# Layer 0's input comes transposed from the host: an fp32 decoder trunk on Trainium2, first tile and first weight chunks in halves

## The chip, the cores and the metric

The kernel runs on one core of one Trainium2 chip. The metric is the device time of one execution in microseconds; the median of three runs of the kernel before is 1779.86 us.

## The reference, cut to what matters

A two-layer decoder trunk in fp32 for 512 prompt positions and 8 x 4 sample positions, 544 rows of 1024 features:

```python
h = x @ w_in        # 2816 columns: 11 pieces of 256 (val, gate, q, k, v, ...)
glu = val * sigmoid(gate)                        # -> causal depthwise conv
A, B, C, D = retention(...), dilated_attention(...), conv_module(glu), spatial_gating(...)
x = LN(alpha * x + concat(A, B, C, D) @ w_out)
x = LN(alpha * x + hier_moe(x))                  # top-1 of 4 groups, top-2 of 8 experts
```

TensorE contracts over partitions, so x @ w_in needs x with its features on the partitions: xT.

## The kernel before

The rows are cut into five tiles (ROWS: four of 128 rows and one of 32). w_in comes in 11 chunks of 1024 KB (128 partitions x 8 feature blocks x 256 columns), w_out in 4 more. They go through a ring of five slots in the big SBUF buffer `arena` (`ring`, `SLOT`); the trace calls the transfers arena<-in_w_proj. Two chunks are mostly used as a pair (`JOBS`), as VAL with GATE and SQ with SK: for each tile and each of the 8 feature blocks one matmul 128x512 (`weigh`, line 595; line 600 for the tile of 32 rows), which the trace shows as two records. xT is one buffer of 8 blocks x 544 positions.

In layer 0 each x tile is loaded with the positions on the partitions (`x_load`, line 373). TensorE transposes its eight 128x128 blocks against an identity into two PSUM banks (`turn_tile`, line 580), ScalarE copies them into xT (`turn_out`, line 1104), and then the VAL/GATE matmuls of that tile run (`first_pair`). The order on TensorE: transposes of tiles 0 and 1, matmuls of tile 0, transposes of tile 2, matmuls of tile 1, and so on. Then `tile(SQ, 0)`, then the transposes of the gating product (line 656), which wait for POOL's `glu` (line 1841), and on.

SyncE issues all loads of weights and x on one queue in the order in which they are written: identity (columns 0 to 127 of `const`), x tiles 0 and 1, chunks VAL and GATE, x tiles 2 to 4, the rest of `const` (lifts `start`), SQ, SK, three pieces of the samples' key cache, then the parameters of the layer, of which ret_state is the last (line 431). POOL waits for `start` ahead of three small scatters (line 1823), and for all five parameter transfers (`par_in`) ahead of two memsets and the gating product, which also waits for ScalarE's last copy of GATE (line 1119). VectorE waits for `start` ahead of everything.

SV and RQ are released when TensorE has finished the last VAL/GATE tile, RK by the SQ/SK job, later cache pieces and chunks by other semaphores of TensorE and VectorE. At the end of the attention part x is loaded again from `x_in`, for the residual sum. The MoE part of each layer streams the experts' matrices of 2048 KB (arena<-in_w, line 490), each released by a matmul of the turn before on the same of three lanes. Layer 1 transposes its x on the chip as well.

## Time and profile before

| | |
|---|---|
| three runs | 1776.07, 1779.86, 1783.07 us |
| span of the profiled execution, first to last instruction | 1777.2 us |
| granted TensorE clock, mean | 0.900 |
| TensorE matmul busy | 1434.9 us (81%) |
| VectorE / ScalarE / POOL busy | 568.8 / 217.3 / 362.6 us |
| 16 DMA engines | 516.25 MB, mean 290 GB/s |

The profiled execution's own device time isn't listed beside its span; the span lies inside the three runs. Times in the trace count from the first instruction of the span. SPq is SyncE's queue, on which the transfers are issued; a transfer lands some time after its issue. PEld is TensorE's loading of the stationary operand, which overlaps the matmuls.

### The profile page before, as it was taken

Reading aid. Unit: us, or ns where it says so; the run is one execution under the profiler, and the core shown is the slowest. Engines: PE = TensorE matmul, PEld = TensorE weight load, DVE = VectorE, ACT = ScalarE, POOL = GpSimd, SP = SyncE. Lnnn points to the kernel's source line nnn. Section 1 sums busy time; section 2 is a strip of 40 time slices with the busy share of each in tenths; the row PEclk is TensorE's granted clock in tenths of the full one; section 3 lists DMA queues with packets and bytes.
Section 4 is the critical chain, followed back from the end, with each engine's and each line's share of the span. In section 5 each row is a group of like instructions: output and inputs, shape, how many; then the busy total and the mean of one; then the engine's idle time right before and its main releaser. Section 6 shows DMA issues by size and latency. Waiting matters only on the chain.

```text
span 1777.2 us, 37861 instructions
## 1 busy us (share of the span) xinstructions
PE 1434.9 (81%) x15465; PEld 880.0 (50%) x15465; DVE 568.8 (32%) x1226; ACT 217.3 (12%) x621; POOL 362.6 (20%) x513
## 2 busy tenths in 40 slices
PE   8989999979567656878498999998757798689870
PEld 4546875555234333445245578746434454355440
DVE  0766654341000000101458756535100011011117
ACT  2223210101000000000022230200000000001000
POOL 1000120023122221323110003110322233224322
PEclk9999999999788787989699999998988899899995
DMA  8242234378999999999850430617799999989993
GB/s 317 86 169 84 72 113 181 132 313 357 425 426 424 426 424 426 400 425 403 323 221 25 169 131 27 228 80 303 322 423 425 420 361 421 424 348 398 419 396 153
DMA packets 60985, 516.25 MB, mean 290 GB/s; under 512 B 12118, under 2 KB 15794, under 8 KB 32122
## 3 DMA queue, kind: packets, MB, share of 16 engines
q1 hardware_dynamic: 49834, 497.47, 68.5%
q0 software_dynamic: 11088, 17.89, 2.8%
q8 instruction: 45, 0.74, 0.2%
q14 instruction: 18, 0.15, 0.0%
HBM read 795.97 MB, written 27.46 MB: 463 GB/s over the span
## 4 chain that ended last, share of the span: by engine, by line
PE 52%; DMA 36%; DVE 6%; issue 2%; SPq 1%; ACT 1%; POOL 1%; POOLq 0%; DVEq 0%; ACTq 0%
DMA arena<-in_w 31%; PE ps L595 22%; PE ps L1036 14%; PE ps L1054 5%; DVE arena L1790 1%; PE ps L600 1%; DMA xT<-x1d,xT 1%; PE ps L700 1%; DMA arena<-in_w_proj 1%; PE ps L580 1%; DMA arena<-in_kv 1%; PE ps L718 1%; PE ps L949 1%; DVE bn L1536 1%; SPq L490 1%
## 5 line engine op out<-in xcount | busy, mean ns | idle before, releaser
L1036 PE MATMUL ps<-arena,xT 128*32 128x256 f32 x7104 | 469.4, 423 | 185.9 <-DMA arena<-in_w 184.6
L1036 PEld LDWEIGHTS ps<-arena,xT 128*32 128x32 f32 x7104 | 273.1, 122 | 369.9 <-issue 268.4
L595 PE MATMUL ps<-arena,xT 128*128 128x512 f32 (+1 forms) x1280 | 446.9, 504 | 2.7 <-DMA arena<-in_w_proj 1.1
L595 PEld LDWEIGHTS ps<-arena,xT 128*128 128x128 f32 x1280 | 245.9, 197 | 176.1 <-issue 152.4
L1758 DVE COPY xT<-ps 128x128 f32<-128x128 f32 x111 | 32.4, 292 | 836.5 <-PE ps L1045 836.5
L1054 PE MATMUL ps<-arena,xT 128*32 128x256 f32 x3552 | 219.0, 387 | 33.3 <-DVE xT L1758 25.5
L1054 PEld LDWEIGHTS ps<-arena,xT 128*32 128x32 f32 x3552 | 112.9, 111 | 111.8 <-issue 29.3
L1879 POOL DMA_INDIRECT xT<-x1d,xT x111 | 116.9, 1053 | 88.1 <-POOL xT L1877 84.8
L1889 POOL DMA_INDIRECT yd<-xT x111 | 113.3, 1021 | 91.4 <-POOL xT L1887 86.4
L1877 POOL COPY xT<-xT 128x1 int32 x111 | 20.5, 185 | 477.4 <-PE ps L1026 477.4
L1310 DVE SCALAR_TENSOR_TENSOR arena<-arena 128x784 f32<-128x784 f32 x120 | 115.3, 1028 | 0.0
L1225 ACT ACTIVATE xT<-ps 128x128 f32<-128x128 f32 x111 | 30.8, 278 | 603.8 <-PE ps L1036 603.8
L1835 POOL TENSOR_TENSOR rstat<-rstat,halfc 128x5 f32<-128x5 f32 (+2 forms) x6 | 14.9, 2484 | 331.2 <-DVE rstat L1272 331.2
L1230 ACT COPY xT<-ps 128x256 f32<-128x256 f32 x111 | 41.4, 373 | 289.9 <-PE ps L1054 289.9
L1116 ACT ACTIVATE arena<-ps 128x256 f32<-128x256 f32 x88 | 31.4, 383 | 301.9 <-PE ps L595 301.9
L580 PE MATMUL ps<-const,arena 128*128 128x128 f32 (+1 forms) x240 | 33.8, 289 | 33.4 <-DVE arena L1545 26.9
L1754 DVE COPY xT<-ps 128x256 f32<-128x256 f32 x117 | 49.7, 425 | 28.4 <-PE ps L1026 28.4
L1026 PE MATMUL ps<-const,xT 128*128 128x128 f32 x234 | 45.6, 277 | 15.2 <-DMA xT<-x1d,xT 14.1
L1863 POOL TENSOR_TENSOR mv<-mv,halfc 128x1 f32<-128x1 f32 (+1 forms) x10 | 15.2, 1519 | 175.0 <-DVE mv L1567 175.0
L580 PEld LDWEIGHTS ps<-const,arena 128*128 128x128 f32 (+1 forms) x240 | 28.6, 154 | 42.1 <-DVE arena L1545 27.9
L1104 ACT COPY xT<-ps 128x512 f32<-128x512 f32 (+1 forms) x50 | 24.8, 525 | 182.4 <-PE ps L580 182.1
L1045 PEld LDWEIGHTS ps<-const,xT 128*128 128x128 f32 x111 | 15.4, 138 | 45.7 <-issue 45.7
(257 smaller groups left out, 1099.5 us busy)
## 6 DMA issues: line engine op xcount, KB each, us to landing
arena<-in_w SPq DMA_DIRECT2D x333, 2048.0 KB
arena<-in_w_proj SPq DMA_DIRECT2D x30, 1024.0 KB, 7.7
arena<-in_kv SPq DMA_DIRECT2D x32, 640.0 KB, 7.5
arena<-yd SPq DMA_DIRECT2D x16, 512.0 KB, 6.9
rowpar<-in_rowpar SPq DMA_DIRECT2D x2, 2708.0 KB, 18.3
arena<-in_x_in SPq DMA_DIRECT2D x8, 512.0 KB, 5.0
x1d<-arena SPq DMA_DIRECT2D x8, 512.0 KB, 2.6
arena<-x1d SPq DMA_DIRECT2D x8, 512.0 KB, 13.3
```

The lines of the kernel that those rows point to most:

```text
L580: ins = pe.transpose(ps[g][:, j * 128:j * 128 + n], source(t, 4 * g + j), ident[0:n, 0:n])
L595: ins = pe.matmul(bank[0:n, 0:w * CW], xT[:, k, 128 * t:128 * t + n], columns(k, slice(0, CW)), start=(k == 0), stop=(k == KT - 1))
L1026: ins = pe.transpose(TOKENS[:, b * 128:(b + 1) * 128], xg[q][:, b * 128:(b + 1) * 128], ident)
L1036: ins = pe.matmul(HB[q][r, 0:256], xgT[q][:, k % 2, BLK * (k // 2):BLK * (k // 2 + 1)], w13[q][:, :, k, 128 * j:128 * (j + 1)], start=(k = ...
L1054: ins = pe.matmul(YB[q][r, 0:256], hT[q][:, BLK * c:BLK * (c + 1)], w2[q][:, c, 256 * t:256 * (t + 1)], start=(c == 0), stop=(c == 3), til ...
L1116: ins = act.activation(h[0:n, c, t, :], bank[0:n, at * CW:(at + 1) * CW], func.get(c, ACT.Copy))
L1230: act.copy(yo[q], YB[q][:, 0:256]).then_inc(sem(f"y_out{q}"), 1)
L1310: ins = dve.scalar_tensor_tensor(out=acc[:, cb, :], in0=src, scalar=cw[:, cb * TAPS + j:cb * TAPS + j + 1], in1=acc[:, cb, :], op0=ALU.mul ...
L1754: dve.tensor_copy(xgT[q], TOKENS[:, 0:256].rearrange("p (b m) -> p b m", b=2)).then_inc(sem(f"xgT{q}"), 1)
L1758: dve.tensor_copy(hT[q], HIDDEN[:, 0:128]).then_inc(sem(f"hT{q}"), 1)
L1879: pool.indirect_dma_start(out=xg[q], out_offset=None, in_=x1q, in_offset=bass.IndirectOffsetOnAxis(ap=gidx[q], axis=0), bounds_check=4 * N ...
L1889: pool.indirect_dma_start(out=ydq, out_offset=bass.IndirectOffsetOnAxis(ap=yidx[q], axis=0), in_=yo[q], in_offset=None, bounds_check=4 * ( ...
```

## The change

The host writes a second copy of x, `xT_in`, already transposed and laid out tile by tile: 128 partitions, and for each tile 8 feature blocks of as many columns as the tile has rows. xT in SBUF takes the same layout for both layers (`xT_tile`). In layer 0 the transposes and ScalarE's copies fall away. x tile 0 comes as two transfers of four feature blocks each, and so do the chunks VAL and GATE. The first halves lift the semaphore `early`, on which the first four matmuls wait; the other four of tile 0 wait for the second halves. `const` is loaded whole, behind SK; TensorE waits for it ahead of `tile(SQ, 0)`. POOL raises the counts of the semaphores of the transposes that fell away. In layer 0, SyncE's wait for the transposes ahead of the fourth cache piece (line 436) goes too. The reload of x for the residual sum stays.

Left out of the diff are lines that only say `xT_tile(t)` in place of a slice of xT (matmuls, router, VectorE's copy), the name of the flat view, and the final count.

```diff
@@ -164,6 +164,7 @@
 
+LOADED = dict(xT_tr=10, xT_low=5, xT_high=5)
 PER = dict(par_in=80, xT_tr=30, xT_low=15, xT_high=15, proj=40, proj_out=40,
@@ -193,7 +194,7 @@
 
-        xT = sb("xT", [128, KT, NTOK])
+        xT = sb("xT", [128, KT * NTOK])
         const = sb("const", [128, sum(n for _, n in const_at.values())])
@@ -207,6 +208,10 @@
         halfc = sb("halfc", [128, 4 * TILES])
+
+        def xT_tile(t):
+            at, n = KT * 128 * t, ROWS[t]
+            return xT[:, at:at + KT * n].rearrange("p (k n) -> p k n", k=KT)
 
@@ -367,13 +372,19 @@
             E = Eng(sp, "none")
-            sp.dma_start(const[:, 0:128], io["const"][:, 0:128]).then_inc(sem("ident"), 16)
-
-            def x_load(t):
-                sp.dma_start(x[0:ROWS[t], t, :], io["x_in"][128 * t:128 * t + ROWS[t], :]).then_inc(sem(f"x_in{t}"), 16)
-
-            x_load(0)
-            x_load(1)
+            HALF = KT // 2
+
+            def xT_load(t, a, b, name):
+                sp.dma_start(xT[:, a:b], io["xT_in"][:, a:b]).then_inc(sem(name), 16)
+
+            def first_half(c):
+                src = io["w_proj"][bass.ds(c, 1), :, 0:HALF * CW].rearrange("a p n -> (a p) n")
+                sp.dma_start(ring[slot(c)][:, 0:HALF].rearrange("p k c -> p (k c)"), src).then_inc(sem("early"), 16)
+
+            def second_half(c):
+                src = io["w_proj"][bass.ds(c, 1), :, HALF * CW:].rearrange("a p n -> (a p) n")
+                sp.dma_start(ring[slot(c)][:, HALF:].rearrange("p k c -> p (k c)"), src).then_inc(sem(f"ring{slot(c)}"), 16)
+
             def ring_fill(layer, c):
@@ -404,11 +415,14 @@
                 if L == 0:
-                    ring_load(0)
-                    ring_load(1)
-                    for t in range(2, TILES):
-                        x_load(t)
-                    sp.dma_start(const[:, 128:], io["const"][:, 128:]).then_inc(start_sem, 16)
+                    xT_load(0, 0, HALF * 128, "early")
+                    first_half(VAL)
+                    first_half(GATE)
+                    xT_load(0, HALF * 128, KT * 128, "x_in0")
+                    second_half(VAL)
+                    second_half(GATE)
+                    for t in range(1, TILES):
+                        xT_load(t, KT * 128 * t, KT * (128 * t + ROWS[t]), f"x_in{t}")
                 else:
@@ -416,6 +430,8 @@
                 ring_load(SK)
+                if L == 0:
+                    sp.dma_start(const[:], io["const"][:]).then_inc(start_sem, 16)
                 for i in range(NKV - 1):
@@ -433,8 +449,8 @@
 
-                        E.need("xT_tr", 2 * TILES)
                         if L:
+                            E.need("xT_tr", 2 * TILES)
                             sp.wait_ge(sem("x_saved"), L * 16 * TILES)
@@ -566,10 +582,9 @@
             ident = C("ident")
-            pe.wait_ge(sem("ident"), 16)
             for L in range(DEPTH):
                 E.L = L
-                turned = [0]
+                turned = [0 if L else TILES]
 
@@ -606,12 +621,18 @@
                     if part != 1:
+                        if j == 0 and L == 0:
+                            pe.wait_ge(sem("early"), 48)
+                            weigh(ps[2], chunks, t, range(KT // 2))
+                            pe.wait_ge(sem("x_in0"), 16)
                         if place == 0:
                     ks = range(KT) if part is None else range(part * KT // 2, (part + 1) * KT // 2)
+                    if j == 0 and L == 0:
+                        ks = range(KT // 2, KT)
                     ins = weigh(ps[2 + j % 2], chunks, t, ks)
@@ -633,22 +654,24 @@
                 def turn_x(t):
-                    pe.wait_ge(*((sem("x2"), (L - 1) * TILES + t + 1) if L else (sem(f"x_in{t}"), 16)))
+                    pe.wait_ge(sem("x2"), (L - 1) * TILES + t + 1)
                     turn_tile(t, x_block)
 
-                turn_x(0)
                 if L:
+                    turn_x(0)
                     first_pair(0)
                         first_pair(t, 1)
+                    first_pair(TILES - 1)
                 else:
-                    for t in range(1, TILES):
-                        turn_x(t)
-                        first_pair(t - 1)
-                first_pair(TILES - 1)
+                    for t in range(TILES):
+                        if t:
+                            pe.wait_ge(sem(f"x_in{t}"), 16)
+                        tile(VAL, t)
+                    pe.wait_ge(start_sem, 16)
                 tile(SQ, 0)
@@ -1094,14 +1117,14 @@
                 E.L = L
-                turned = [0]
+                turned = [0 if L else TILES]
 
                         src = ps[g][:, :].rearrange("p (j m) -> p j m", j=4)[:, :, 0:n]
-                        E.done(act.copy(xT[:, 4 * g:4 * g + 4, 128 * t:128 * t + n], src), ("xT_low", "xT_high")[g])
+                        E.done(act.copy(xT_tile(t)[:, 4 * g:4 * g + 4, :], src), ("xT_low", "xT_high")[g])
                     turned[0] += 1
@@ -1120,11 +1143,15 @@
 
-                for t in range(TILES):
-                    turn_out(t, (0, 1))
-                    if t:
-                        proj_out(VAL, t - 1)
-                proj_out(VAL, TILES - 1)
+                if L:
+                    for t in range(TILES):
+                        turn_out(t, (0, 1))
+                        if t:
+                            proj_out(VAL, t - 1)
+                    proj_out(VAL, TILES - 1)
+                else:
+                    for t in range(TILES):
+                        proj_out(VAL, t)
                 for t in range(TILES):
@@ -1809,6 +1836,8 @@
 
+            for name, n in LOADED.items():
+                pool.sem_inc(sem(name), n)
             pool.sem_inc(sem("yidx"), 1)
@@ -1967,8 +1996,10 @@
     colpar = c(np.concatenate([col[n].reshape(L, 128, -1) for n, _ in COLPAR], 2)).reshape(L * 128, -1)
+    rows_in = np.concatenate([a["x_prompt"].reshape(SEQ, D), a["x_sample"].reshape(NS, D)], 0)
+    xT_in = [rows_in[128 * t:128 * t + n].reshape(n, KT, 128).transpose(2, 1, 0).reshape(128, KT * n) for t, n in enumerate(ROWS)]
     return dict(
-        x_in=c(np.concatenate([a["x_prompt"].reshape(SEQ, D), a["x_sample"].reshape(NS, D)], 0)),
+        xT_in=c(np.concatenate(xT_in, 1)), x_in=c(np.concatenate([a["x_prompt"].reshape(SEQ, D), a["x_sample"].reshape(NS, D)], 0)),
         w_proj=w_proj, kv=kv.reshape(L * 16, 128, 2 * NKEY), rowpar=rowpar, colpar=colpar, router_w=router_w,
```

TensorE, from the start of the program. Before (x_in0 to x_in4 are the x tiles, ring0 and ring1 the slots of VAL and GATE, xT_low and xT_high ScalarE's copies):

```order
L580 MATMUL ps<-const,arena 128x128 [waits x_in0,ident]
L580 MATMUL ps<-const,arena 128x128 x7
L580 MATMUL ps<-const,arena 128x128 [waits xT_low,x_in1]
L580 MATMUL ps<-const,arena 128x128 x3
L580 MATMUL ps<-const,arena 128x128 [waits xT_high]
L580 MATMUL ps<-const,arena 128x128 x3
L595 MATMUL ps<-arena,xT 128x512 [waits ring0,ring1,xT_high,xT_low]
L595 MATMUL ps<-arena,xT 128x512 x7
L580 MATMUL ps<-const,arena 128x128 [waits xT_low,x_in2]
```

And with the change (its line 610 is line 595 of before, 615 is 600):

```order
L610 MATMUL ps<-arena,xT 128x512 [waits early]
L610 MATMUL ps<-arena,xT 128x512 x3
L610 MATMUL ps<-arena,xT 128x512 [waits ring1,ring0,x_in0]
L610 MATMUL ps<-arena,xT 128x512 x3
L610 MATMUL ps<-arena,xT 128x512 [waits x_in1]
L610 MATMUL ps<-arena,xT 128x512 x7
L610 MATMUL ps<-arena,xT 128x512 [waits proj_out,x_in2]
```

The transposes are gone, tile 0 is cut in two by its waits, and the other tiles wait for their x alone (and for the PSUM bank).

SyncE's queue, from its start. Before:

```order
L370 DMA const<-in_const 128x128
L373 DMA arena<-in_x_in 128x1024 x2
L379 DMA arena<-in_w_proj 128x2048 x2
L373 DMA arena<-in_x_in 128x1024 x2
L373 DMA arena<-in_x_in 32x1024
L411 DMA const<-in_const 128x2982
L379 DMA arena<-in_w_proj 128x2048
L379 DMA arena<-in_w_proj 128x2048 [waits pinit]
L404 DMA arena<-in_kv 128x1280 x3
```

And with the change:

```order
L378 DMA xT<-in_xT_in 128x512
L382 DMA arena<-in_w_proj 128x1024 x2
L378 DMA xT<-in_xT_in 128x512
L386 DMA arena<-in_w_proj 128x1024 x2
L378 DMA xT<-in_xT_in 128x1024 x3
L378 DMA xT<-in_xT_in 128x256
L390 DMA arena<-in_w_proj 128x2048
L390 DMA arena<-in_w_proj 128x2048 [waits pinit]
L434 DMA const<-in_const 128x3110
L415 DMA arena<-in_kv 128x1280 x3
```

The first transfers are now the ones of the first four matmuls; the constants have moved behind SQ and SK.

## Rows read from the trace of the kernel before

**Rows 1.** The page, its part 2: matmul busy tenths in 40 slices.
```profile
PE   8989999979567656878498999998757798689870
```
**Rows 2.** Chain of waits, first 60 us: start us, us, what.
```profile
2.57 8.75 DMA arena<-in_w_proj
...
11.45 9.10 PE ps L595 x16
20.55 0.87 PE ps L580 x8
21.43 6.87 PE ps L595 x16
28.30 0.87 PE ps L580 x8
29.17 6.87 PE ps L595 x16
36.04 0.61 PE ps L580 x8
36.65 7.06 PE ps L595 x16
43.72 1.89 PE ps L600 x64
45.60 7.06 PE ps L595 x16
52.66 0.45 PE ps L656 x4
```
**Rows 3.** Timeline of SyncE's queue, first issues: start us, us, engine, line, operation.
```profile
0.71 0.39 SPq L370 DMA_DIRECT2D const<-in_const  x1
1.16 0.90 SPq L373 DMA_DIRECT2D arena<-in_x_in  x2
```
**Rows 4.** DMA issues: x loads of line 373, and the identity (last figure: landing).
```profile
DMA to landing us min/median/max: 3.9/9.5/11.1
...
const<-in_const SPq DMA_DIRECT2D x1, 64.0 KB, 2.0
```
**Rows 5.** Busy time by stretch: engines, then granted clock, DMA share, GB/s.
```profile
2.00:3.00 1.00, 0.00 (x0) 0.00 (x0) 0.00 (x0) 0.00 (x0) 1.00 (x1) 1.00 0.90 145
...
6.00:11.00 5.00, 3.05 (x14) 2.27 (x12) 0.00 (x0) 3.53 (x5) 0.00 (x0) 1.00 1.00 418
```
**Rows 6.** Timeline of TensorE's weight loads in tile 0 of VAL/GATE.
```profile
15.00 0.34 PEld L595 LDWEIGHTS ps<-arena,xT 128*128 128x128 f32 x1 [0.52 <-issue]
15.67 0.19 PEld L595 LDWEIGHTS ps<-arena,xT 128*128 128x128 f32 x1 [0.34 <-issue]
16.10 0.19 PEld L595 LDWEIGHTS ps<-arena,xT 128*128 128x128 f32 x1 [0.24 <-issue]
```
**Rows 7.** Timeline of TensorE at the start of layer 1.
```profile
875.97 1.97 PE L580 MATMUL ps<-const,arena 128*128 128x128 f32 x8 [20.50 <-DVE arena L1545]
878.66 8.99 PE L595 MATMUL ps<-arena,xT 128*128 128x512 f32 x16 [0.72 <-issue]
```
**Rows 8.** Timeline of POOL and ScalarE, 18 to 54 us.
```profile
18.59 0.10 POOL L1819 MEMSET nowhere<- 128x1 int32 x1 [14.29 <-DMA const<-in_const]
...
39.17 0.15 POOL L1838 MEMSET arena<- 128x60 f32 x1 [15.78 <-DMA arena<-in_ret_state]
39.37 0.53 POOL L1839 MEMSET arena<- 128x512 f32 x1
47.56 2.88 POOL L1841 TENSOR_TENSOR arena<-arena 128x1280 f32<-128x1280 f32 x1 [7.66 <-ACT arena L1119]
...
45.67 1.81 ACT L1119 ACTIVATE arena<-ps 32x64 f32<-32x64 f32 x8 [1.26 <-PE ps L600]
```
**Rows 9.** Expert stage of layer 0: stretch (as rows 5), and a link of the chain.
```profile
400.00:860.00 460.00, 331.49 (x4836) 187.24 (x4828) 41.44 (x148) 32.23 (x99) 119.72 (x195) 0.85 0.99 413
...
444.22 37.30 DMA arena<-in_w
```

More of the change, by code:

```diff
@@ L483, in _ @@
                 E.need("stores", 16 * 9)
-                E.need("xT_tr", 20)
+                E.need("xT_tr", 4 * TILES)
                 E.need("smp_back", 1)
@@ L594, in weigh @@
                         if t < TILES - 1:
-                            ins = pe.matmul(bank[0:n, 0:w * CW], xT[:, k, 128 * t:128 * t + n], columns(k, slice(0, CW)),
+                            ins = pe.matmul(bank[0:n, 0:w * CW], xT_tile(t)[:, k, :], columns(k, slice(0, CW)),
                                             start=(k == 0), stop=(k == KT - 1))
@@ L948, in tile_logits @@
                     for k in range(KT):
-                        ins = pe.matmul(ps[6][0:n, t * NLOG:(t + 1) * NLOG], xT[:, k, 128 * t:128 * t + n], rw[:, k, :],
+                        ins = pe.matmul(ps[6][0:n, t * NLOG:(t + 1) * NLOG], xT_tile(t)[:, k, :], rw[:, k, :],
                                         start=(k == 0), stop=(k == KT - 1))
@@ L1915, in _ @@
                     E.done(pool.tensor_tensor(mv[0:n, t, 2:3], mv[0:n, t, 3:4], halfc[0:n, 0:1], ALU.pow), "x2_pow")
-    wrong = {name: (made.get(name, 0), n) for name, n in PER.items() if made.get(name, 0) != n * DEPTH}
+    wrong = {name: (made.get(name, 0), n) for name, n in PER.items() if made.get(name, 0) != n * DEPTH - LOADED.get(name, 0)}
     assert not wrong, wrong
```

6 lines of the change are left out of this document (3 added, 3 removed).

## The prediction

> **What bounds the kernel now.** I read the page's slices first. TensorE is busy in nine or eight tenths of nearly every slice, so no single stage stands out at a glance [rows 1]. The question is therefore only what the start-up costs and whether time saved there reaches the end. The chain of waits answers the first half [rows 2]: from 2.57 us the chain waits 8.75 us for the second weight chunk (landing at 11.32), and from 11.45 us it is TensorE without a break: five VAL/GATE tiles with the transposes of tiles 2, 3 and 4 between them, to 45.60, where the SQ/SK job begins. The chain has no ACT, POOL or DMA link between 11.45 and 52.66. So two things can be won: the wait ahead of 11.45 and the transposes inside the stretch. The two transposes ahead of 11.45 (tiles 0 and 1) lie under the wait for the weights and are worth nothing.
>
> The queue of SyncE shows why the weights land so late: the identity (64 KB) is issued at 0.71 and two x tiles from 1.16 on, ahead of the two chunks of 1024 KB [rows 3]. Sizes in KB are of 1024 bytes.
>
> **Term 1, when TensorE can start.** After the change it needs half of x tile 0 (256 KB) and two half chunks (512 KB each): 1280 KB = 1.311 MB, the first transfers in the queue. No row shows this transfer, so I bound it with two landings. x tile 0 landed 3.9 us after its issue at 1.16, at 5.06, with 64 + 512 KB = 0.590 MB asked for up to it [rows 3, 4]. The second chunk landed at 11.32 with 64 + 2 x 512 + 2 x 1024 KB = 3.211 MB [rows 2]. Between them 2.621 MB in 6.26 us: 0.419 MB/us, which is the 418 GB/s of the stretch from 6 to 11 us [rows 5]. On that line 1.311 MB lands at 5.06 + 0.721/0.419 = 6.78 us. The line holds the identity's cost: from 2 to 3 us the DMA engines were 0.90 busy and moved only 145 GB/s [rows 5], rows of 512 bytes; at 418 the same bytes take 0.35, so up to 0.65 us falls away, and I take 0.3. Bounds: 5.9 (all of it falls away, and a little of the interleaving behind x tile 0) and 6.9. I take **6.5**, and 0.13 us to the first matmul as now (11.32 to 11.45): 6.63.
>
> **Term 2, the first tile.** Its matmuls (two records each, 16 in all) start 0.85 us apart at first and 0.43 from 15.67 on [rows 6]: five records at TensorE's lower level of 1.2 GHz, eleven at 2.4, 9.10 us in all [rows 2], though the column of the granted clock says 1.00 there. Did the transposes of tiles 0 and 1 ahead of it help to raise the clock? At the start of layer 1 TensorE had been idle for 20.50 us, did only the 1.97 us of transposes and then the same tile in 8.99 us [rows 7]. Less work ahead, the same tile: I take 9.10 with nothing ahead of it. Bounds: 7.03, the 16 records all at 0.43 and the drain (a clock already high, for which nothing speaks), and 13.7, sixteen at 0.853. The second half of the tile waits for 2.621 MB (x tile 0 and both chunks whole): on the line 5.06 + 2.031/0.419 = 9.9 us. Its first half takes five records of 0.853 and three of 0.43, 5.56 us, to 12.2, so that wait costs nothing; if the clock were high at once, the first half would end at 10.1, and still no wait. Tile 0 ends at 6.63 + 9.10 = 15.73 instead of 20.55: **4.82 us**.
>
> **Term 3, the transposes in the stretch.** 0.87 + 0.87 + 0.61 = **2.35 us** go [rows 2]. What stays is 6.87 + 6.87 + 7.06 + 1.89 = 22.69. The x tiles that these wait for are issued after the halves: tile 1 is the 3.145th MB, 11.2 us on the line, and tile 4 the 4.325th, 14.0; TensorE asks at 15.7 and at 36.5. The five pairs of ScalarE's copies out of PSUM go too; they hid under matmuls. The SQ/SK job then starts at 15.73 + 22.69 = 38.42 instead of 45.60: **7.18 us** earlier.
>
> **What has moved behind it.** The constants, identity included, now stand behind SQ and SK. Their bytes and those ahead of them: x 2176 KB, four chunks 4096 KB, constants 1555 KB, together 7827 KB = 8.01 MB, 5.06 + 7.42/0.419 = 22.8 us. Readers: TensorE at 38.4 (a new wait, with 15 us to spare), VectorE not before its first copy (after 52.66 now), and POOL, whose three small scatters now follow at 18.59 [rows 8] and then idle for ret_state. All hidden. SyncE still waits for two of POOL's memsets ahead of SK, which are POOL's first work and no later than before. SQ and SK land by 19, before 38.4. SyncE issues two transfers more (three halves and no identity), some 0.45 us each as the first ones [rows 3]; it is far ahead of the DMA engines by then.
>
> ret_state is the last of the parameters, at 39.17 [rows 8], and the bytes ahead of it are the same: it stays at 39.1, because it is the DMA engines that set it. POOL then does its two memsets (0.15 and 0.53) and is free at 39.9. It needs ScalarE's last copies of GATE: now 45.67 + 1.81 = 47.5, then 40.3. So the gating product starts at 40.3 and ends 2.88 later at 43.2, and TensorE wants it at 52.66 - 7.18 = 45.48. Slack 2.3 us, as now (50.4 to 52.66). This is the one place where the fixed DMA time and the earlier TensorE meet; ret_state could be 1.5 us later and still cost nothing at all on TensorE.
>
> The new layout of xT, tile by tile, keeps each 128x128 block contiguous per partition; the copies and weight loads have the same shapes. I cost it at nothing: a weight load of 0.19 us lies under a matmul of 0.43 [rows 6].
>
> **Does it reach the end?** After 52.66 every transfer of layer 0 is released by a semaphore of TensorE or VectorE, and moves with it. The expert stage is where it could be lost: from 400 to 860 us the DMA engines are 0.99 busy at 413 GB/s, and the chain goes through loads of up to 37.30 us [rows 9]. But the load issued before 444.22 was released by a matmul of the turn before, and the streamed bytes are fixed: a stream that starts 7.18 us sooner ends 7.18 us sooner. So the sum is 4.82 + 2.35 = 7.2 us (0.4%) off the profiled execution with its span of 1777.2, which lies within the three runs shown (median 1779.86). From the median: 1779.86 - 7.2 = **1772.7**.
>
> **Rivals.**
> A, the halves don't overlap. The lone 64 KB transfer took 2.0 us from issue to landing [rows 4]; if each of the three early pieces paid that in series, they would land at 0.71 + 6.0 + 1.311/0.419 = 9.8, tile 0 would end at 19.1, and the gain would be 3.8: 1776.1. Against it: x tiles and chunks, issued 0.45 apart, moved at a steady 418 GB/s [rows 5]. Chance 0.06. The Trainium skill speaks for this rival, "DMA: Bandwidth & Descriptors", section Bandwidth: transfers should be batched to a mebibyte or more, and the fit on the same page (2.0 us + bytes at 436 GB/s each) would give the three in series 9.0 us, so a landing at 9.7, an estimate from that page. The trace disagrees so far as it goes, with its 418 GB/s over queued transfers of 512 and 1024 KB.
> B, the clock stays low through the first tile, since nothing precedes it: 16 x 0.853 = 13.65, 4.55 more, gain 2.6: 1777.2. Against it the restart [rows 7]. Chance 0.12 with what lies halfway.
> C, all goes well: landing at 5.9, clock up after three records, gain 7.2 + 0.6 + 0.9 = 8.7, and up to 9.6 if the second half's landing (9.9, and 3.4 of matmuls) sets it: 1770.3 to 1771.2. Chance 0.10.
> D, the gain is absorbed downstream: the expert stage waits on bytes, and if its stream were already at its limit before its first turn, nothing would arrive: 1779.9. Against it: its loads wait for TensorE's turns. Chance 0.10. This is also how it looks if scatter covers it, since the runs before span 7.0 us by themselves.
> E, slower. The new pieces (rows of 1 to 4 KB out of longer rows) move as badly as the identity did, 145 GB/s instead of 418: 4.325 MB take 29.8 us instead of 10.3, so ret_state lands at 58.6, the gating product ends at 58.6 + 0.8 + 2.88 = 62.3, and TensorE, which now wants it at 52.66, stands: 9.6 us lost, 1789.5. It decides from a ret_state later than 52.66 - 2.88 - 0.8 = 49.0, which is 214 GB/s for those pieces. Against it: the present x tiles already are rows of 4 KB, at 418. Chance 0.03.
>
> **The numbers.** My forecast has 0.59. The gain is set beside a median of runs that lie 7.0 us apart, so I allow 2 to 3 us on either side of the cases: **1768.5 to 1777.5** takes in A, B and C and leaves out most of D and E. A measurement of this kernel can tell about 0.5% from no change, 8.9 us. Faster by more: C with luck, and the forecast with scatter, 0.21. Slower by more: E, 0.03. Within: 0.76.
>
> **What the changed profile would show.** First matmul near 6.6 us; records 0.85 apart for some 4 us, then 0.43; no pause between the halves; SQ/SK starting near 38.4; POOL's product ending before TensorE asks (no wait of matmuls at the transposes of VAL); ret_state still at 39; the first experts some 7 us sooner. I would be wrong if TensorE waited for POOL near 45 us, if the first tile took over 11 us, or if the stage from 400 us did not move with the start.

## The result and the profile after

The changed kernel takes 1765.55 us (median of 4 runs, 1764.52 to 1768.49), and the kernel before, taken beside it, 1779.59 (4 runs, 1776.07 to 1783.07): a ratio of 0.9919, 95% interval 0.9898 to 0.9940, so 14 us or 0.8% faster. The forecast was 1772.7 with 1768.5 to 1777.5. The sign is right, and the size is about half of what came: 7.2 us forecast, 14 measured. The profiled execution took 1764.52 us, with a span of 1762.7. One run of the kernel of experiment 10 took 2785.49 us where its five others took 1765.42 to 1768.04; it is left out below.

The page, its first part and the matmul slices of part 2, stand like this after the change; matmuls are busy 1422.3 us where the trace of before has 1434.9:

```profile
span 1762.7 us, 37770 instructions
...
PE 1422.3 (81%) x15425; PEld 871.3 (49%) x15425; DVE 568.5 (32%) x1226; ACT 212.5 (12%) x611; POOL 360.3 (20%) x513
...
PE   8989999888577656887498999998857798599880
```

**The start.** The chain of waits of the changed kernel (start us, us, what) answers to [rows 2]:

```profile
1.63 6.55 DMA arena<-in_w_proj
...
8.22 29.32 PE ps L610 x64
37.54 1.88 PE ps L615 x64
39.43 7.06 PE ps L610 x16
46.49 0.45 PE ps L679 x4
```

The halves land at 8.18 and the first matmul starts at 8.22 instead of 11.45. From there TensorE runs without a break and the SQ/SK job starts at 39.43 instead of 45.60: 6.17 us earlier, where 7.18 were forecast. The four full tiles take 29.32; without 6.87 + 6.87 + 7.06 for tiles 1 to 3 [rows 2], tile 0 took 8.52. That the tiles 1 to 3 are as before is seen on ScalarE, whose copies of the tiles out of PSUM now follow each other at 6.87 us (before 7.75 and 7.67, with the transposes between):

```profile
30.71 0.66 ACT L1139 ACTIVATE arena<-ps 128x256 f32<-128x256 f32 x2 [6.21 <-PE ps L610]
37.58 0.66 ACT L1139 ACTIVATE arena<-ps 128x256 f32<-128x256 f32 x2 [6.21 <-PE ps L610]
```

The landing is late because the DMA engines move less than they did. Busy time by stretch of the changed kernel (PE, PEld, DVE, ACT, POOL, then granted clock, DMA share, GB/s), beside [rows 5]:

```profile
3.00:4.00 1.00, 0.00 (x0) 0.00 (x0) 0.00 (x0) 0.00 (x0) 1.00 (x3) 1.00 0.91 270
4.00:5.00 1.00, 0.00 (x0) 0.00 (x0) 0.00 (x0) 0.00 (x0) 0.30 (x1) 1.00 0.77 283
5.00:6.00 1.00, 0.00 (x0) 0.00 (x0) 0.00 (x0) 0.00 (x0) 0.00 (x0) 1.00 0.98 338
6.00:11.00 5.00, 2.78 (x4) 1.23 (x5) 0.00 (x0) 0.00 (x0) 0.00 (x0) 1.00 0.97 318
```

From 6 to 11 us it is 318 GB/s, where the kernel before moved 418 in the same stretch. The engines are nearly as busy (0.97 and 1.00): they are not short of work, each piece takes longer.

The weight loads of tile 0 answer to [rows 6] (timeline: start us, us, engine, line, operation, in brackets the idle time ahead):

```profile
9.23 0.34 PEld L610 LDWEIGHTS ps<-arena,xT 128*128 128x128 f32 x1 [0.52 <-issue]
10.09 0.34 PEld L610 LDWEIGHTS ps<-arena,xT 128*128 128x128 f32 x1 [0.52 <-issue]
10.94 0.34 PEld L610 LDWEIGHTS ps<-arena,xT 128*128 128x128 f32 x1 [0.52 <-issue]
11.63 0.19 PEld L610 LDWEIGHTS ps<-arena,xT 128*128 128x128 f32 x1 [0.35 <-issue]
```

Records 0.85 apart at first, the level of 1.2 GHz, and from 11.63 on 0.43, that of 2.4 GHz, four such records instead of five. TensorE had done nothing at all ahead of them. From 12.06 on all of them stand 0.43 apart, so there is no pause between the first halves and the second.

**What moved behind it.** POOL and ScalarE, 18 to 46 us, beside [rows 8]:

```profile
25.56 0.10 POOL L1848 MEMSET nowhere<- 128x1 int32 x1 [21.27 <-DMA const<-in_const]
...
40.33 0.15 POOL L1867 MEMSET arena<- 128x60 f32 x1 [9.97 <-DMA arena<-in_ret_state]
40.54 0.52 POOL L1868 MEMSET arena<- 128x512 f32 x1
41.38 2.88 POOL L1870 TENSOR_TENSOR arena<-arena 128x1280 f32<-128x1280 f32 x1 [0.33 <-ACT arena L1142]
```
```profile
39.50 1.81 ACT L1142 ACTIVATE arena<-ps 32x64 f32<-32x64 f32 x8 [1.26 <-PE ps L615]
```

The constants land at 25.56, forecast 22.8, both well ahead of 39.4. ret_state lands at 40.33, 1.2 later than forecast; POOL's product ends at 44.26, and TensorE asks at 46.49. The slack is 2.2 us, as before.

**Where the rest of the 14 us comes from.** The table sets the same matmuls side by side in both traces (start us in each):

| TensorE's instruction | before | after | earlier by |
|---|---|---|---|
| SQ/SK job of tile 0 | 45.60 | 39.43 | 6.2 |
| its next transposes of the gating product | 52.66 | 46.49 | 6.2 |
| end of the retention stage, layer 0 (L913, now L936) | 249.84 | 241.93 | 7.9 |
| first expert's transposes (L1026, now L1049) | 378.03 | 368.88 | 9.2 |
| last product of layer 0's experts (L1054, now L1077) | 852.01 | 841.90 | 10.1 |
| first transposes of layer 1 | 875.97 | 864.36 | 11.6 |
| gating transposes of layer 1 (L656, now L679) | 922.61 | 910.29 | 12.3 |
| the same retention matmul in layer 1 | 1119.91 | 1105.04 | 14.9 |
| end of the span | 1777.2 | 1762.7 | 14.5 |

In this pair of traces the start's 6.2 us arrive whole, and another 8 come in steps behind it, at places that the change does not touch. The retention stage of layer 0 shows best what they look like. First the kernel before, its timeline of TensorE:

```profile
219.44 5.41 PE L595 MATMUL ps<-arena,xT 128*128 128x256 f32 x16
...
227.94 3.72 PE L595 MATMUL ps<-arena,xT 128*128 128x256 f32 x16
...
233.79 5.41 PE L595 MATMUL ps<-arena,xT 128*128 128x256 f32 x16
```

and the changed one:

```profile
212.25 5.41 PE L610 MATMUL ps<-arena,xT 128*128 128x256 f32 x16
...
220.74 3.72 PE L610 MATMUL ps<-arena,xT 128*128 128x256 f32 x16
...
226.60 3.72 PE L610 MATMUL ps<-arena,xT 128*128 128x256 f32 x16
...
234.44 6.53 PE L610 MATMUL ps<-arena,xT 128*128 128x256 f32 x16
241.93 1.99 PE L936 MATMUL ps<-arena 128*128 128x256 f32 x8
```

The same sixteen records take 3.72 us or 5.41 and up to 6.53, and which of them are slow differs between the traces. The granted clock says why. Busy time by stretch, before:

```profile
212.00:219.00 7.00, 7.00 (x96) 5.95 (x95) 5.42 (x11) 0.86 (x4) 1.12 (x1) 0.76 0.46 150
219.00:226.00 7.00, 7.00 (x30) 5.82 (x29) 5.22 (x8) 0.38 (x1) 7.00 (x4) 0.76 0.01 2
232.00:239.00 7.00, 7.00 (x80) 5.88 (x78) 6.81 (x9) 0.39 (x3) 1.24 (x1) 0.76 0.00 0
```

and after, 7.2 us earlier. The work of the first stretch has a full clock here, that of the second a low one again, and that of the third, now at 225 to 232 us, a full one (1.00 from 226 to 232 too); a low one comes behind it:

```profile
205.00:212.00 7.00, 7.00 (x104) 5.86 (x104) 5.15 (x11) 0.86 (x4) 0.00 (x0) 1.00 0.40 129
212.00:219.00 7.00, 7.00 (x29) 5.81 (x29) 5.98 (x11) 0.38 (x1) 6.82 (x4) 0.76 0.06 25
219.00:226.00 7.00, 7.00 (x81) 5.93 (x82) 2.70 (x9) 0.38 (x1) 2.03 (x3) 1.00 0.04 12
232.00:240.00 8.00, 8.00 (x23) 4.96 (x22) 5.14 (x11) 0.00 (x0) 4.06 (x2) 0.58 0.55 192
```

TensorE was wholly busy in all of these stretches (7.00 of 7.00, 8.00 of 8.00), so the clock did not fall for want of work in them. Over the whole execution its mean is 0.900 before and 0.911 after.

A slow group costs only what lies on the path that ends last. The step from 6.2 to 7.9 us in this stage is in the sum not the clock but a wait: in the kernel before TensorE stands 2.30 us for VectorE at line 913, in the changed one (`241.93` above) it doesn't.

```profile
249.84 2.68 PE L913 MATMUL ps<-arena 128*128 128x256 f32 x8 [2.30 <-DVE arena L1281]
```

Just ahead of it the changed kernel is 5.5 us earlier (the matmuls before that instruction start at 240.90 and 246.44), so its slow groups had cost more than those of before. But the one of 6.53 us lies where TensorE would have stood for VectorE, whose step ends at 241.43, and so costs about half a microsecond here and not 2.8. In layer 1 it is the other way round: there the changed kernel has the wait and the one before hasn't, and the gain still grows by 2.6 us.

```profile
1105.04 1.99 PE L936 MATMUL ps<-arena 128*128 128x256 f32 x8 [2.30 <-DVE arena L1308]
```

The wait in layer 0 is no work of the change either: it stands in 17 of the 19 traces of this case, in all nine of kernels without the change and in all five others with its early start.

The last turn of layer 0's experts is the same kind of thing as the slow groups (3.46 us at 852.01 before, 1.93 at 841.90 after, for 32 matmuls each; the granted clock is 0.61 from 852 to 856 and 1.00 from 840 to 845). Another of the places is a wait for POOL. In layer 1 of the kernel before, TensorE stands 0.93 us for POOL's product, because ret_state lands late there, which it doesn't do after:

```profile
918.98 0.15 POOL L1838 MEMSET arena<- 128x60 f32 x1 [15.52 <-DMA arena<-in_ret_state]
```
```profile
922.61 1.09 PE L656 MATMUL ps<-const,arena 128*128 128x128 f32 x8 [0.93 <-POOL arena L1841]
```
```profile
906.36 0.15 POOL L1867 MEMSET arena<- 128x60 f32 x1 [14.52 <-DMA arena<-in_ret_state]
```
```profile
910.29 1.04 PE L679 MATMUL ps<-const,arena 128*128 128x128 f32 x8
```

Two single executions can't tell a shift that belongs to the change from one that any two executions have. That is what the experiments are for.

### The profile page after: what moved, and what is told of

Its sections match the earlier page's. It is cut to its first block, busy times and chain, and to the rows that moved or that the text cites. A ratio compares the mean times of both kernels' runs of the same rounds, so it can differ in the third digit from the quotient of the medians.

```text
span 1762.7 us, 37770 instructions
## 1 busy us (share of the span) xinstructions
PE 1422.3 (81%) x15425; PEld 871.3 (49%) x15425; DVE 568.5 (32%) x1226; ACT 212.5 (12%) x611; POOL 360.3 (20%) x513
## 4 chain that ended last, share of the span: by engine, by line
PE 53%; DMA 37%; DVE 6%; issue 2%; ACT 1%; SPq 1%; POOL 0%; POOLq 0%; DVEq 0%; ACTq 0%
DMA arena<-in_w 33%; PE ps L610 24%; PE ps L1059 14%; PE ps L1077 4%; PE ps L615 1%; PE ps L723 1%; PE ps L595 1%; DMA xT<-x1d,xT 1%; DMA arena<-in_kv 1%; DMA arena<-in_w_proj 1%; DVE arena L1817 1%; PE ps L972 1%; PE ps L741 1%; SPq L506 1%; PE ps L733 1%
## 5 line engine op out<-in xcount | busy, mean ns | idle before, releaser
L1077 PE MATMUL ps<-arena,xT 128*32 128x256 f32 x3552 | 217.2, 385 | 30.9 <-DVE xT L1785 24.8
L1077 PEld LDWEIGHTS ps<-arena,xT 128*32 128x32 f32 x3552 | 112.3, 110 | 108.8 <-DVE xT L1785 28.5
L1864 POOL TENSOR_TENSOR rstat<-rstat,halfc 128x5 f32<-128x5 f32 (+2 forms) x6 | 14.9, 2484 | 329.2 <-DVE rstat L1299 329.2
L1049 PE MATMUL ps<-const,xT 128*128 128x128 f32 x234 | 45.5, 277 | 12.8 <-DMA xT<-x1d,xT 11.7
L595 PE MATMUL ps<-const,arena 128*128 128x128 f32 (+1 forms) x200 | 27.3, 283 | 27.0 <-DVE arena L1572 27.0
L1127 ACT COPY xT<-ps 128x512 f32<-128x512 f32 (+1 forms) x40 | 19.9, 523 | 182.1 <-PE ps L595 181.7
L595 PEld LDWEIGHTS ps<-const,arena 128*128 128x128 f32 (+1 forms) x200 | 23.2, 152 | 33.3 <-DVE arena L1572 27.7
```

Source lines behind the costliest of these rows:

```text
L595: ins = pe.transpose(ps[g][:, j * 128:j * 128 + n], source(t, 4 * g + j), ident[0:n, 0:n])
L1049: ins = pe.transpose(TOKENS[:, b * 128:(b + 1) * 128], xg[q][:, b * 128:(b + 1) * 128], ident)
L1077: ins = pe.matmul(YB[q][r, 0:256], hT[q][:, BLK * c:BLK * (c + 1)], w2[q][:, c, 256 * t:256 * (t + 1)], start=(c == 0), stop=(c == 3), til ...
```

## The experiments

Means and standard errors over all runs of a kernel are worked out from the single times. The kernel before: 1779.8 (141 runs, one run scatters by 3.1 us around it; the means of the six batches that were taken beside the other kernels lie between 1778.1 and 1780.1). The changed kernel: 1766.6 +- 0.5 (9 runs). Where nothing else is said a diff is against the changed kernel.

**1. The layout alone.** The kernel before, with xT tile by tile and nothing else.

```diff
-        xT = sb("xT", [128, KT, NTOK])
+        xT = sb("xT", [128, KT * NTOK])
...
-                            ins = pe.matmul(bank[0:n, 0:w * CW], xT[:, k, 128 * t:128 * t + n], columns(k, slice(0, CW)),
+                            ins = pe.matmul(bank[0:n, 0:w * CW], xT_tile(t)[:, k, :], columns(k, slice(0, CW)),
```

> The kernel before, with xT laid out tile by tile in both layers and nothing else changed: x still comes untransposed, TensorE still transposes it. The first 46 us explain 6.2 us of the 14 gained, so 8 are open. Theory S (what comes after the start depends only on when SQ/SK starts, and the rest of the gain is where the clock drops and VectorE's wait fall): no change, 1779 +-3, first matmul at 5.2, SQ/SK at 45.6. Theory L (the layout makes matmuls or copies cheaper): 8 us faster, 1771, most of it in layer 1 as well.

Measured: 1780.58 (12 runs), ratio 1.0012 [0.9996, 1.0027]. The layout brings no gain: the mean is 1781.9, 2.0 +- 0.9 slower than the kernel before.

**2. Without the halves.** x tile 0, VAL and GATE each in one transfer, one wait for them.

```diff
-                    xT_load(0, 0, HALF * 128, "early")
-                    first_half(VAL)
-                    first_half(GATE)
-                    xT_load(0, HALF * 128, KT * 128, "x_in0")
-                    second_half(VAL)
-                    second_half(GATE)
+                    xT_load(0, 0, KT * 128, "x_in0")
+                    ring_load(VAL)
+                    ring_load(GATE)
...
-                            pe.wait_ge(sem("early"), 48)
-                            weigh(ps[2], chunks, t, range(KT // 2))
                             pe.wait_ge(sem("x_in0"), 16)
...
-                    if j == 0 and L == 0:
-                        ks = range(KT // 2, KT)
```

> The changed kernel with x tile 0 and the chunks VAL and GATE loaded whole again, no halves. If the halves do what they are for, the first matmul starts later than 8.2: on my line (2.621 MB without the identity) at 9.7, SQ/SK at 40.9, total 1767. Rival: the pieces of 2 and 4 KB of the halves are what slowed the first transfers (283 to 338 GB/s instead of 418), then the whole transfers cost nothing or little: first matmul at 8.2 to 9, total as the changed kernel, 1765.5.

Measured: 1768.32 (6 runs), ratio 0.9933 [0.9908, 0.9957]. The chain:

```profile
1.63 7.96 DMA arena<-in_w_proj
...
9.72 30.25 PE ps L607 x64
```

Twice the bytes land at 9.59 (1.63 + 7.96), only 1.4 us later than the halves, and the stretches show the rate that the halves gave up:

```profile
3.00:4.00 1.00, 0.00 (x0) 0.00 (x0) 0.00 (x0) 0.00 (x0) 1.00 (x3) 1.00 1.01 410
4.00:5.00 1.00, 0.00 (x0) 0.00 (x0) 0.00 (x0) 0.00 (x0) 0.30 (x1) 1.00 1.04 438
5.00:6.00 1.00, 0.00 (x0) 0.00 (x0) 0.00 (x0) 0.00 (x0) 0.00 (x0) 1.00 1.00 418
```

Whole transfers: 410 to 438 GB/s from 3 us on. Halves: 270 to 338, and 201 to 360 in the second profile of the changed kernel (experiment 4). Of the 6.17 us at the start, the halves bring 1.5 (first matmul at 8.22 and not at 9.72). The means of all runs, 1767.9 +- 1.2 and 1766.6 +- 0.5, fit that, but their difference is within the scatter.

**3 and 6. The start held back.** The first matmul waits for x tile 1 as well, which brings the SQ/SK job back to about where it was; everything else is as changed. Below this is the held kernel.

```diff
                             pe.wait_ge(sem("early"), 48)
+                            pe.wait_ge(sem("x_in1"), 16)
```

> The changed kernel, but TensorE's first matmul also waits for x tile 1, which landed about 14 us in. SQ/SK then starts at about 45.2, as in the kernel before (45.6), while all else of the change stays. Theory S: everything behind hangs on that start, so 1779 +-3, and the retention stages of both layers look as before (four low windows of the clock ahead of layer 0's experts, the 2.3 us wait for VectorE). Theory L or any other that has the 8 us in something else of the change: 1771.5.

> The changed kernel held back to x tile 1, once more. Theory C: the median moves towards that of the kernel before, 1776 or more, since the first median was luck. Theory S2: 1772 +-2 again, and the profile (the first one was of the slowest of eleven runs) shows in which stages the 7 us lie: I expect the retention stage of layer 1 at 47.7 us and the end of layer 0's experts some 3 us shorter.

Measured: 1772.16 (11 runs), ratio 0.9956 [0.9939, 0.9972], and 1774.22 (12 runs), 0.9967 [0.9954, 0.9979]; mean of the 23 is 1773.2 +- 0.7. The chain of the first of them, with SQ/SK at 45.87, 0.27 later than in the kernel before:

```profile
14.38 29.60 PE ps L610 x64
...
45.87 7.06 PE ps L610 x16
```

This is the run that divides the result. Giving back the early start (39.43 and 40.80 in two profiles of the changed kernel, 45.87 and 46.24 here: 5.9 us) costs 6.6 +- 0.9 us, so within that error it reaches the end one to one. But 6.6 +- 0.7 us less than before remain with no early start at all: SQ/SK starts even later here than in the two profiles of the kernel before (45.60, and 44.96 in experiment 5).

**4 and 5. The same kernels again**, unedited, for a second profile and more runs.

> The changed kernel once more, as it is, for a second profile. If the places at which the clock drops hang on the timing of the work, they lie where they lay (93, 213, 233 us and 957, 1076 us) and the run takes 1765.5 +-2. If they are chance, they lie elsewhere, and the time in the stretch from 195 to 250 us differs by 1.7 us per window of low clock.

> The kernel before, unchanged, for a second profile. Between equal starts of SQ/SK (hold and before) the medians differ by 7.5 us, though the two profiled runs differ by 1. Theory C (chance of where the clock's low windows fall, the same for every kernel): 1779.7 +-2, and the retention stage of layer 1 takes 50.2 us in some profiles and 47.7 in others. Theory S2 (something of the change shifts them for good): the same 50.2 us again here.

Measured: changed 1767.09 (5 runs), 0.9928 [0.9905, 0.9952]; before 1780.87 (10 runs) beside 1780.49 (35), 1.0006 [0.9994, 1.0019]. The result stands. In the second profile of the changed kernel (span 1765.3) TensorE's slow stretches lie elsewhere in layer 0, and its first tile is slower: 30.62 us for the four tiles instead of 29.32. Where the clock falls isn't fixed by the program. The second profile of the kernel before (span 1781.1) has its first tile in 8.52 us instead of 9.10, and SQ/SK at 44.96.

**7. Constants late.** The kernel before, with the bulk of the constants behind SK, as the change has it.

```diff
-                    sp.dma_start(const[:, 128:], io["const"][:, 128:]).then_inc(start_sem, 16)
...
                 ring_load(SK)
+                if L == 0:
+                    sp.dma_start(const[:, 128:], io["const"][:, 128:]).then_inc(start_sem, 16)
```

> The kernel before with the bulk of the constants loaded behind SK instead of ahead of SQ, the identity still first, nothing else changed. Theory S2 in the form that the order of the loads matters (POOL's scatters and its semaphore for VectorE come later): up to 7 us faster, 1773. Otherwise no change, 1779.7 +-2.

Measured: 1779.77 (12 runs), 0.9995 [0.9985, 1.0005]. The mean is 0.8 +- 0.6 us below the kernel before, nothing that could carry 6.6.

**8. The other inputs' place in HBM.** The kernel before, given the new input xT_in without reading it.

```diff
+    rows_in = np.concatenate([a["x_prompt"].reshape(SEQ, D), a["x_sample"].reshape(NS, D)], 0)
+    xT_in = [rows_in[128 * t:128 * t + n].reshape(n, KT, 128).transpose(2, 1, 0).reshape(128, KT * n) for t, n in enumerate(ROWS)]
...
-        x_in=c(np.concatenate([a["x_prompt"].reshape(SEQ, D), a["x_sample"].reshape(NS, D)], 0)),
+        xT_in=c(np.concatenate(xT_in, 1)), x_in=c(np.concatenate([a["x_prompt"].reshape(SEQ, D), a["x_sample"].reshape(NS, D)], 0)),
```

> The kernel before, with the transposed copy of x present as a first input that nothing reads. It only moves the addresses of all the other inputs in HBM by 2.2 MB. If the placement in HBM is what makes the changed kernel faster behind its start (the expert stages stream 333 matrices from there), 7 us faster, 1772. Otherwise no change, 1779.7 +-2.

Measured: 1778.33 (12 runs), 0.9996 [0.9980, 1.0012]. The mean is 0.7 +- 1.2 us below the kernel before, again too little.

**9 and 10. The wait for POOL's product in layer 1.** POOL makes the gating product ahead of its wait for the parameters and its two memsets; once in the kernel before (9), once in the changed one (10).

```diff
+                E.need("proj_out", job(GATE, 4) + 1)
+                E.done(pool.tensor_tensor(h[:, VAL], h[:, VAL], h[:, GATE], ALU.mult), "glu")
                 E.need("par_in", 80)
...
                 E.done(pool.memset(QB, 0.0), "ctx_pool")
-                E.need("proj_out", job(GATE, 4) + 1)
-                E.done(pool.tensor_tensor(h[:, VAL], h[:, VAL], h[:, GATE], ALU.mult), "glu")
```

> The kernel before, with POOL's gating product ahead of its wait for the parameters and of the two memsets (in both layers). In five profiles of kernels with the start of before, TensorE waits 0.4 to 1.4 us in layer 1 for that product, because ret_state lands 1.2 us later there than in the five profiles with the changed start, where it never waits. Theory G (this wait, and the place of the low windows behind it, is where the rest of the gain comes from): no wait in layer 1, 1780.3 falls by 1 to 5 us. Theory C (other low windows make it up): within 1 us of 1780.

> The changed kernel with the same move of POOL's product. It doesn't wait for it as it is, in either layer, so theory G says: 1766.5 +-1.5, no gain. It would be the kernel to keep if it is not slower.

Measured: 1780.39 (12 runs), 0.9998 [0.9981, 1.0016], and 1767.09 (5 runs), 0.9919 [0.9890, 0.9947]. The wait is gone from the profile of 9, whose product starts ahead of ret_state:

```profile
915.52 2.90 POOL L1838 TENSOR_TENSOR arena<-arena 128x1280 f32<-128x1280 f32 x1 [13.62 <-ACT arena L1119]
918.34 0.16 POOL L1840 MEMSET arena<- 128x60 f32 x1
```
```profile
920.47 1.04 PE L656 MATMUL ps<-const,arena 128*128 128x128 f32 x8
```

and the mean is 0.1 +- 1.0 us below the kernel before. So this wait doesn't carry the 6.6 us, though it looked like a cause in the pair of traces; whether its own 0.93 us reach the end is below what these runs can tell.

**11 to 16, 18. The length of TensorE's stream.** The change takes 40 transposes out of TensorE's instructions. So small matmuls (4x4, on zeros, into a bank that isn't used yet) were put in front, under the wait for the first load: 20 and 64 in the changed kernel, 44 (twice) and 64 in the kernel before, 20 in the held one, and 20 with ten small ScalarE copies in the held one.

```diff
             ident = C("ident")
+            pe.wait_ge(sem("pinit"), 3)
+            for _ in range(20):
+                pe.matmul(ps[7][0:4, 0:4], h[0:4, 0, 4, 0:4], h[0:4, 1, 4, 0:4], start=True, stop=True)
```

> The changed kernel with 20 matmuls of 4x4 (two records and two weight loads each, 80 instructions) ahead of its first one, while TensorE waits for data: its instruction stream is then as long as before the 40 transposes were removed. Theory F (the 16 KB packet of the instruction queue that takes a DMA engine for 1.03 us at 11.2 us behind the parameters' issue, at 11.6 in the changed kernel, hangs on the position in TensorE's stream, and delays ret_state when it comes at 11.2): ret_state lands 11.3 us after its issue in layer 1 as before instead of 10.1, TensorE waits for the product again, and the time rises by 2 to 7 us, to 1769 to 1773. Rival (the position of the stream doesn't matter): 1766.5 +-1.5 and 10.1 us.

> The kernel before with 44 matmuls of 4x4 (176 instructions) ahead of its first transposes. If the stream is fetched in blocks of 16 KB (256 instructions of 64 bytes, an estimate from the packet's size), 176 more puts every later instruction where 80 fewer would, as in the changed kernel. The start of VAL/GATE may come up to 1 us later, as x tile 0's transposes begin later. Theory F: ret_state lands 10.1 us after its issue in layer 1, no wait for the product there, total 1774 to 1778. Rival: 1780 to 1781 and 11.3 us.

> The changed kernel with 64 matmuls of 4x4 (256 instructions) ahead of its first one, in the wait for data. Theory F (only the position of the later instructions within blocks of 16 KB counts): the same position as without any, so 1766.6 +-1, while 20 of them gave 1768.7. Rival P (the matmuls themselves cost, by holding up the start or the clock): slower than with 20, 1770 or more. Rival C (neither; the 2 us were chance): 1766 to 1769.

> The kernel before with 64 of them. Theory F: its own position again, so no gain of 4 us: 1780, and up to 1.5 us more since the transposes of x tile 0 start later. Rival P' (the gain of 44 came from what they do to the start, a first tile in 8.1 us instead of 9.1): 1776 to 1778 again.

> The changed kernel held back to x tile 1, with 20 of them: start of SQ/SK and position in TensorE's stream both as in the kernel before. If these two are all there is, 1780 +-1.5. If the position counts only for the 2 us seen so far, 1775.3 +-1.5, and 4 to 5 us of the gain stay without a cause.

> The kernel before with 44 of them, once more. Theory F and rival P' both say 1776 +-1.5; 1779 or more says that the first result was chance.

For the last one the edit in ScalarE is

```diff
-            act.wait_ge(sem("pinit"), 2)
+            act.wait_ge(sem("pinit"), 3)
+            for k in range(10):
+                act.copy(small[0:4, 24 + 4 * k:28 + 4 * k], h[0:4, 0, 4, 0:4])
```

> The changed kernel held back to x tile 1, with 20 small matmuls on TensorE and 10 small copies on ScalarE in front. If the length of ScalarE's stream carries the 4 to 5 us that are left: 1779 to 1781. If not: 1775.2 +-1.5, and they stay open.

| kernel | added | median (runs) | ratio to before | mean, and against its base |
|---|---|---|---|---|
| changed | 20 matmuls | 1769.16 (6) | 0.9928 [0.9902, 0.9953] | 1768.7, +2.1 |
| changed | 64 | 1768.71 (6) | 0.9933 [0.9917, 0.9949] | 1769.0, +2.4 |
| before | 44 | 1775.95 (12) | 0.9978 [0.9959, 0.9996] | 1776.7 for both, -3.1 |
| before, again | 44 | 1776.52 (10) | 0.9987 [0.9973, 1.0001] | |
| before | 64 | 1779.87 (11) | 0.9993 [0.9978, 1.0008] | 1780.7, +0.9 |
| held | 20 | 1776.02 (12) | 0.9977 [0.9964, 0.9990] | 1775.2, +2.0 |
| held | 20, and 10 on ScalarE | 1774.54 (12) | 0.9980 [0.9966, 0.9994] | 1774.6, +1.4 |

With work of no use ahead of the first matmul the end moves by -3.1 to +2.4 us. In the kernel before, 44 small matmuls make it faster, though they put off the first transposes from 5.17 to 6.69 us and the first tile from 11.45 to 11.79. Part of that is at the start, where they shorten the first tile:

```profile
4.35 2.34 PE ps L571 x88
...
11.79 8.09 PE ps L598 x16
```
```profile
11.79 7.37 PE ps L598 x16
```

(the first run of it, then the second; 9.10 in [rows 2], 8.52 in the second profile of the kernel before.) SQ/SK starts at 44.93 and 44.20 there, against 45.60 and 44.96: 0.7 us early on average, of 3.1 in all, so some 2.4 us come behind. In the changed kernel the small matmuls end ahead of the first landing, and SQ/SK starts at 39.75 and 40.06 with them, between the 39.43 and 40.80 without; their 2 us come behind it. With 64 the small matmuls end later, the first tile starts at 12.79 and takes 8.89, and the total is that of before. One theory was that the place of the instructions in the blocks in which they are fetched matters, by which 64 more, a whole block, change nothing. The kernel before would allow it (+0.9, with an error of 1.2), the changed one not (+2.4, with an error of 0.9, and as much as with 20). It falls in this form, and so does its path through a late ret_state: with 20 more the changed kernel is slower without waiting for POOL's product in layer 1, and with 44 more the kernel before is faster and still waits 0.56 us for it in the first of its two profiles. Ten copies in ScalarE's stream make no difference that can be seen (0.6 +- 1.0 us less). What remains is a difference between kernels that differ only in work of no use: 2.2 +- 0.7 us for the two changed ones together, 1.7 +- 0.8 for the two held ones, -3.1 +- 0.7 for the kernel before with 44. Where behind the start it arises wasn't found. It may bear on about a third of the 6.6 us; that is not shown.

## Why the prediction was wrong in size and right in direction

- **What bounds the kernel now**, and that the wait for the weights and the three transposes in the stretch are all there is to win at the start: right.
- **Term 1** took a landing at 6.5 (bounds 5.9 to 6.9); it was 8.18, outside its bounds. The line through two landings at 0.419 MB/us was taken from transfers that came whole, and the small pieces don't move on it. The same line gave 9.9 for the bytes of experiment 2, and 9.59 was measured: the line was right, and using it for halves was not. What failed is the bound from above, for which the forecast had only the slack of the identity; a third off the rate should have stood there. The rival in which the halves don't overlap (a landing at 9.8) and the estimate of 9.7 from the page of the Trainium skill ("DMA: Bandwidth & Descriptors", section Bandwidth, that transfers should be batched to a mebibyte or more) lie above the measured 8.18, and the forecast below. That estimate takes a fit which the page gives for single transfers issued from GpSimd (section Anatomy of one DMA); those here are issued by SyncE, and several are in flight. The trace agrees with the page's direction: halves of 512 KB moved at 270 to 338 GB/s, whole chunks at 410 to 438.
- **Term 2**: 4.82 from a start at 6.63 and a tile of 9.10. The tile took 8.52 here and 9.8 in the second profile (30.62 less 20.80). So 9.10 was fair (the kernel before itself has 8.52 in its second profile), and the rival of a low clock through the whole tile (13.65) didn't come in any profile.
- **Term 3**: 2.35 us gone, as said: the tiles follow each other at 6.87 us with nothing between them.
- Together 6.2 instead of 7.2 at the SQ/SK job. Between the second profiles of the two kernels it is 4.2 (44.96 and 40.80), so 5.2 on average: the start gave less than forecast.
- **What has moved behind it**: no wait for the constants, none for POOL's product, slack 2.2 instead of 2.3. Right, with the landings 1 to 3 us later than forecast (ret_state 1.2, constants 2.8, x tile 1 3.0 in the held kernel), which fits the lower rate of the halves.
- **Layout, constants' order**: costed at nothing, and no gain in experiments 1 and 7.
- **Does it reach the end?** That it is carried one to one is borne out: 5.9 us at the start were 6.6 +- 0.9 at the end between the held and the changed kernel. The sentence that failed is the next one, "So the sum is 4.82 + 2.35 = 7.2 us". It takes every stage behind 52.66 as the same work at the same clock, and so puts all of the change but its early start at nothing. The changed kernel, its start held back, is still 6.6 us faster than the one before (1773.2 +- 0.7 against 1779.8). Layout, constants' order, place of the inputs and the wait in layer 1 don't carry it: tried one by one in the kernel before, they add up to 0.4 +- 2.1 us slower. That the miss is no larger is luck, as the start fell short by 1 to 2 us while this came on top.
- The cause of these 6.6 us is **open**. Some 2 are of the size that useless matmuls in front make by themselves, and a part goes with the clock. Two profiles of each kernel show it poorly (mean 0.911 and 0.914 in the changed kernel, 0.900 twice in the one before, 0.900 and 0.905 in the held one), but it is on record for every run: 0.9054 on average before (137 runs), 0.9072 held (23), 0.9096 changed (9), with an error of 0.0011 for the last two. Among the runs of the kernel before, a mean clock higher by 0.01 goes with 6.2 us less. An estimate from this slope gives the held kernel's clock 1.1 +- 0.7 of its 6.6 us. Why its clock is higher isn't known.
- SyncE's wait for the transposes ahead of the fourth cache piece, which goes too, cost nothing: in the kernel before the piece is issued at 46.03, right behind chunk SV at 45.66, and the transposes were done by 36.65; in the changed one the two stand at 39.86 and 39.49. Not tried: the transposes and ScalarE's copies taken away by themselves, with x still coming as before.
- **The range** allowed 2 to 3 us of scatter on the median and nothing for an effect behind the start of the opposite kind to the one in the rival of absorption. The largest gain in any case was C's 8.7 to 9.6, all of it at the start, and faster than the range had a chance of 0.21. A gain behind the start, from anything else that the change does, had no case at all; a kernel whose granted clock is not full (0.85 in the expert stage, [rows 9]) should have had one.

No experiment beats the changed kernel: with POOL's product ahead (10) it is 1767.09 (5 runs), the same.

## What to carry to other kernels

A wait removed at the very start, with everything behind released by semaphores, arrived at the end one to one here (5.9 us as 6.6 +- 0.9): check it with a kernel that only adds the wait back, since that also shows what else the change did. Halving first loads to start early pays less than the bytes say, as the halves moved at two thirds of the rate of whole transfers: half of the bytes landed only 1.4 us sooner, where the line through whole transfers gave 3.1. Where a pair of traces shows a tidy cause far behind the edit (here 0.93 us of waiting in layer 1), remove it in the kernel before and time it; here that moved the mean by 0.1 +- 1.0 us. And builds that differ only in work of no use lay 2 to 3 us apart, so a gain of that size at the end isn't evidence for any one cause. Before a slow group is counted, see whether the engine would have waited there anyway: 2.8 us of low clock cost half a microsecond at line 913.

## What the runs showed of the hardware that was not expected

- Halves of rows moved slower than whole ones while several such transfers were queued: 270 to 338 GB/s from 3 to 11 us at a DMA share of 0.77 to 0.98, against 410 to 438 at 1.00 to 1.04 for whole ones (experiment 2). Worked out from the single records, packets of 4096 bytes took 159 ns in the median, but those that started from 2 to 9 us in the changed kernel took 173 to 255 on average, microsecond by microsecond, so some take far longer. Those of 8192 bytes in experiment 2 took 309 in the median and 309 to 321 on average. The size of the packet alone isn't it: x tiles with packets of 4096 bytes took 159 to 160 on average from 4 us on in the kernel before, and 159 to 161 from 10 us on in the changed one. What it is wasn't tried.
- The granted clock falls in stretches of full TensorE work (0.76 from 212 to 219 us with 7.00 of 7.00 us busy), and not in the same places in two executions of one kernel. A run of the kernel before scatters by 3.1 us, of the changed one by 1.5; the medians of 17 to 35 runs of the kernel before lie between 1777.43 and 1780.49. Runs with a mean clock higher by 0.01 are 6.2 us faster (137 runs of the kernel before).
- 44 useless 4x4 matmuls under the wait for the first weights made the kernel before 3.1 +- 0.7 us faster, 64 of them didn't (0.9 +- 1.2 slower).
- The first tile took 9.10 us behind two tiles of transposes [rows 2] and 8.52 in a second execution, and with nothing ahead of it 8.52 in one execution and 9.8 in another: work ahead of the first matmul isn't needed for TensorE to reach 2.4 GHz within it, and when it does so varies.
